# Scan stage of a two-block model: two jobs of ScalarE's strand are given to VectorE

## The reference

```python
def _ssd_chunked(x, dt, log_a, bm, cm):        # chunks of 128 tokens, 8 heads of 64, 2 groups, state 128
    xdt = (x * dt[..., None]).reshape(n, nc, q, h, p)
    acs = jnp.cumsum(log_a.reshape(n, nc, q, h), axis=2)
    seg = acs_h[..., :, None] - acs_h[..., None, :]
    lmat = jnp.exp(jnp.where(tril, seg, -jnp.inf))
    scores = jnp.einsum('nclhd,ncshd->nhcls', c_h, b_h) * lmat
    y_diag = jnp.einsum('nhcls,ncshp->nclhp', scores, xdt)
    ...
    return (y_diag + y_off).reshape(n, t, h, p)

y = unboth(_ssd_chunked(both(xs, xs), ...))    # forward and reversed
y = y + ssd_d.astype(f32)[:, None] * xs        # the D product, per head
```

## Time and profile before

| what | value |
|---|---|
| three runs | 2898.67, 2905.77, 2908.02 us |
| median | 2905.77 us |
| the profiled execution | 2908.02 us, its span 2906.2 us |
| TensorE, VectorE, ScalarE, GpSimd busy | 95%, 59%, 40%, 7% of the span |
| mean granted TensorE clock | 0.974 of full |

### The profile page before, as it was taken

How to read it: one execution, slowest core, us unless ns; L and a number is a source line. 1 busy time by engine, 2 the same in 40 slices (tenths; PEclk the granted TensorE clock), 3 DMA queues, 4 the chain that set the end, 5 groups by cost and what they waited for, 6 DMA issues and landing times.

```text
span 2906.2 us, 41919 instructions
## 1 busy us (share of the span) xinstructions
PE 2748.0 (95%) x16930; PEld 2095.4 (72%) x16930; DVE 1717.6 (59%) x3101; ACT 1163.1 (40%) x2102; POOL 211.3 (7%) x212
## 2 busy tenths in 40 slices
PE   7999997889999999999988999999999998999998
PEld 4888766775766666666645776888888775788887
DVE  4256876665677777767647787533333688433333
ACT  3332654222255565555522328422223327432222
POOL 0000000000011222221200020000000030000000
PEclk9999897999999999999999999999999999999999
DMA  6210001434368899999976340313323250222311
GB/s 234 87 58 23 1 1 47 122 91 157 145 262 341 345 347 354 347 352 342 360 283 233 98 113 1 123 59 128 97 69 121 86 130 15 88 87 86 124 63 69
DMA packets 186543, 442.39 MB, mean 152 GB/s; under 512 B 21284, under 2 KB 110695, under 8 KB 167015
## 3 DMA queue, kind: packets, MB, share of 16 engines
q1 hardware_dynamic: 161862, 396.59, 37.9%
q0 software_dynamic: 24480, 43.04, 5.0%
HBM read 426.43 MB, written 38.29 MB: 160 GB/s over the span
## 4 chain that ended last, share of the span: by engine, by line
PE 78%; DVE 8%; DMA 7%; ACT 4%; issue 2%; POOL 0%; SPq 0%; POOLq 0%; ACTq 0%; DVEq 0%
PE ps L296 18%; PE ps L298 18%; PE ps L297 18%; PE ps L2514 6%; DMA ring<-in_ew 3%; DMA hg<-h_rows,idx 2%; PE ps L2030 2%; PE ps L1514 2%; PE ps L2540 1%; PE ps L2753 1%; PE ps L2234 1%; DVE Pb L3500 1%; PE ps L586 1%; DMA yr<-y_rows 1%; PE ps L3386 1%
## 5 line engine op out<-in xcount | busy, mean ns | idle before, releaser
L2965 DVE TENSOR_TENSOR wf<-ring,wf 128x1024 fp32r<-128x1024 f32 (+1 forms) x152 | 181.6, 1196 | 310.8 <-ACT wf L2961 310.5
L2961 ACT ACTIVATE wf<-ring 128x1024 fp32r<-128x1024 f32 (+1 forms) x152 | 156.8, 1033 | 346.3 <-PE ps L298 346.3
L296 PE MATMUL ps<-hxh,wf 128*128 128x512 f32 (+1 forms) x736 | 279.9, 380 | 2.3 <-DVE hxl L3128 2.3
L297 PE MATMUL ps<-hxl,wf 128*128 128x512 f32 (+1 forms) x736 | 279.5, 380 | 0.0
L298 PE MATMUL ps<-hxh,wf 128*128 128x512 f32 (+1 forms) x736 | 279.5, 380 | 0.0
L2452 DVE TENSOR_TENSOR spA<-ring,spA 128x1024 fp32r<-128x1024 f32 x156 | 184.3, 1220 | 104.9 <-ACT spA L2447 104.8
L2514 PE MATMUL ps<-ring,hdT 128*128 128x512 f32 x520 | 234.8, 594 | 0.8 <-issue 0.8
L2447 ACT ACTIVATE spA<-ring 128x1024 fp32r<-128x1024 f32 x156 | 157.7, 1053 | 57.3 <-DMA ring<-in_ew 50.1
L2452 DVE TENSOR_TENSOR spB<-ring,spB 128x1024 fp32r<-128x1024 f32 x104 | 123.8, 1220 | 70.1 <-ACT spB L2447 70.1
L2514 PEld LDWEIGHTS ps<-ring,hdT 128*128 128x128 f32 x520 | 93.8, 190 | 94.3 <-issue 91.2
L296 PEld LDWEIGHTS ps<-hxh,wf 128*128 128x128 f32 x736 | 138.4, 188 | 29.0 <-DVE hxl L3128 2.8
(11 more groups left out here) (622 smaller groups left out, 6148.8 us busy)
## 6 DMA issues: line engine op xcount, KB each, us to landing
ring<-in_ew SPq DMA_DIRECT2D x65, 2048.0 KB, 12.2
ring<-in_ew SPq DMA_DIRECT2D x65, 1024.0 KB
ring<-in_w_in SPq DMA_DIRECT2D x17, 2048.0 KB, 7.9
ring<-in_w_gate SPq DMA_DIRECT2D x20, 1024.0 KB, 5.5
ring<-in_w_up SPq DMA_DIRECT2D x20, 1024.0 KB, 8.1
ring<-in_w_down SPq DMA_DIRECT2D x16, 1024.0 KB, 5.0
adaw<-in_ada_w SPq DMA_DIRECT2D x24, 512.0 KB, 6.6
ring<-in_w_out SPq DMA_DIRECT2D x6, 2048.0 KB, 8.0
```

The lines of the kernel that those rows point to most:

```text
L296: pe.matmul(o, lhs[0], rhs[0], start=start, stop=False)
L297: pe.matmul(o, lhs[0], rhs[1], start=False, stop=False)
L2961: act.activation(item_part(n)[0], item_raw(n), ACT.Copy).then_inc(*w_hi.inc(n))
L2965: v.tensor_tensor(item_part(n)[1], item_raw(n), f(item_part(n)[0]), ALU.subtract).then_inc(*w_lo.inc(n))
```

## The change

Both jobs leave ScalarE's strand. VectorE makes `lax` with one multiply of 128x1024 (`g128` repeated for 8 heads, times the head's log decay repeated along 128 columns), and the D product with one multiply of 128x512 into the buffer `yo`, which is free once L1037 has read it; x is no longer overwritten. The signals follow: TensorE waits for `lx` from VectorE, and VectorE no longer waits for ScalarE's D product.

```diff
@@ ssd_pe
-                pe.wait_ge(*PA.val(((i - 1, d), "lx")))
+                pe.wait_ge(*PV.val(((i - 1, d), "lx")))
@@ ssd_act
-                if i < 4:
-                    act.wait_ge(*PV.val((u, "xdt")))
-                    for h in range(8):
-                        o = B["xst"][:, 64 * h:64 * h + 64]
-                        m = act.activation(o, o, ACT.Copy, scale=sdd[:, h:h + 1])
-                    m.then_inc(*PA.inc((u, "xd")))
                 yield
                 yield
-            if 1 <= i < 5:
-                at = 16 * ORD[d][i + 1] + 8 * d
-                for h in range(8):
-                    m = act.activation(B["lax"][:, 128 * h:128 * h + 128], C(f"g128_{d}"), ACT.Copy, scale=las[:, at + h:at + h + 1])
-                m.then_inc(*PA.inc((u, "lx")))
@@ ssd_dve
                 if i < 4:
                     v.tensor_tensor(ydst, bA[:, :], yo_, ALU.add).then_inc(*PV.inc((u, "ys")))
                     v.wait_ge(*PV.val((u, "ys")))
-                    v.wait_ge(*PA.val((u, "xd")))
+                    v.tensor_tensor(h8(yo_), h8(xst), bc(sdd[:, :], 64), ALU.mult).then_inc(*V.inc())
+                    v.wait_ge(*V.val())
...
-                v.tensor_tensor(ydst, ydst, xst if i < 4 else yo_, ALU.add).then_inc(*PV.inc((u, "yd")))
+                v.tensor_tensor(ydst, ydst, yo_, ALU.add).then_inc(*PV.inc((u, "yd")))
...
+            if 1 <= i < 5:
+                la = las[:, 16 * ORD[d][i + 1] + 8 * d:16 * ORD[d][i + 1] + 8 * d + 8]
+                v.tensor_tensor(lax.rearrange("p (h s) -> p h s", h=8), bcm(C(f"g128_{d}"), 8), bc(la, 128),
+                                ALU.mult).then_inc(*PV.inc((u, "lx")))
             if x:
                 yield
```

More of the change, by code:

```diff
@@ L902, in _program @@
     s_pe = [Signal(sem(f"ssd_mm{d}"), ssd_keys(d, "xT ex bT ~seg0 ~seg1 ~y ~o st", "bT st")) for d in range(2)]
-    s_act = [Signal(sem(f"ssd_scalar{d}"), [k for k in ssd_keys(d, "xst ex btk ~e0 ~e1 ~xd lx", "btk lx") if k != ((0, d), "lx") and (k[1] != "xd" or k[0][0] < 4)]) for d in range(2)]
-    s_dve = [Signal(sem(f"ssd_vector{d}"), ssd_keys(d, "~gt xdt xde ~sc0 ~sc1 ~yo ~ys ~yd H", "xde H")) for d in range(2)]
+    s_act = [Signal(sem(f"ssd_scalar{d}"), ssd_keys(d, "xst ex btk ~e0 ~e1", "btk")) for d in range(2)]
+    s_dve = [Signal(sem(f"ssd_vector{d}"), [k for k in ssd_keys(d, "~gt xdt xde ~sc0 ~sc1 ~yo ~ys ~yd lx H", "xde lx H")
+                                            if k != ((0, d), "lx")]) for d in range(2)]
     def ssd_pe(pe, d):
@@ L974, in ssd_act @@
         for i in range(6):
-            u, pu, x = (i, d), (i - 1, d), i >= 2
+            u, pu = (i, d), (i - 1, d)
             act.wait_ge(*P.val((u, "xT")))
```

## The result

The changed kernel took 2916.55 us (median of 5, 2914.11 to 2920.84) beside 2902.02 us (5 runs, 2896.44 to 2908.02) for the kernel before. The ratio of their fast runs is 1.0052, 95% interval 1.0040 to 1.0064, so 11.6 to 18.6 us slower. The profiled execution took 2919.35 us (span 2917.6), 11.3 us more than the one of before. The forecast of 2916.0 holds in sign and time. The difference was forecast at 10.2 us; it is 14.5 by the two medians, and most of what follows is about the part that was missing. That the time itself came within 0.6 us is luck in part: it was counted from 2905.77 us, the median of three runs of before, and that of five is 3.75 us lower, about as much as the difference came out too small.

What follows compares the result with a forecast made beforehand. VectorE was taken to set the scan stage's time until TensorE takes over near 369 us. Terms 0.8 + 3.1 + 3.1 + 2.3 = 9.3 us, plus 0.9 for TensorE's clock, gave 10.2 us: 2916.0 us, range 2907 to 2924.

Steps and rivals of the forecast that it cites:

- What bounds the stage: Scan stage: VectorE sets the time from 355.14 until TensorE takes over near 369 us; ScalarE's removed bursts are worth zero.
- The products: On VectorE: 1.13 us for each of eight `lax` multiplies, 0.72 us for each of four D multiplies.
- the dear end of 2.34 us: Upper bound for one `lax` product on VectorE, if two broadcasts should cost; 8.5 us more in the sum.
- Rounds 2 and 3: Units i = 2 and 3, both products in each direction on VectorE: 3.11 us longer each.
- Round 4: Unit i = 4, `lax` products only, no wait in direction 1: 2 x 1.13 = 2.26 us longer.
- Unit 1: Two `lax` products on VectorE, the first starting in its 0.83 us wait before L1052: 0.8 us longer.
- TensorE's clock: New TensorE lulls before L927 and L1101 may drop its clock: 0.3 us for each of three rounds, 0.9 in all.
- The bounds of 0 and 6: Range of the clock term: 0, or 2 us a round, 6 in all, if the clock stays low at L1101, L935 and L1104.
- The heavy price: By the skill's rule on recurring gaps, each of three rounds pays for a fallen clock: the 6 us bound, 2921.1 us.
- The sum: Whole stage: 0.8 + 3.1 + 3.1 + 2.3 = 9.3 us without the clock, 10.2 us with its 0.9.
- Rival 3: TensorE's clock falls in every round and costs in full: 9.3 + 6 = 15.3 us, 2921.1 us; chance 15%.
- Rival 2: The 1.64 us wait at a round's end takes back part of the additions: 3.6 us, 2909.4 us; chance 16%.

Runs made afterwards that it cites:

- `lax` alone: Kernel before with only the `lax` product moved to VectorE, the D product left on ScalarE: 2916.98 us, ratio 1.0046 to before.
- `lax` ahead of the wait: Changed kernel with the `lax` product issued ahead of VectorE's wait for the output matmuls in units 2 to 4: 2912.66 us, ratio 1.0027 to before.
- D alone: Kernel before with only the D product moved to VectorE, `lax` left on ScalarE: 2908.24 us, ratio 1.0018 to before.

## Why the forecast was right, and where it was not

*What bounds the stage:* right. Steps added between VectorE's waits count in full (D: +1.70 us for 1.7 expected), a step removed comes back in full (-4.35), and ScalarE's L1002 bursts are worth 0.0 us in the periods.

*The products:* right. 1.13 for `lax`, 0.73 for D; the dear end of 2.34 us for two broadcast inputs is out. The Trainium skill ("VectorE: DVE Perf Modes", The DRAIN you can't avoid) would have the neighbour wait until the pipe is empty, and adds that an instruction which nothing holds may start earlier; the traces show the second: 1.13 or 1.14 us after the start of an instruction of 1.22, behind every one of these products.

*Rounds 2 and 3:* 3.1 us each, measured 3.11 and 3.12 with the clock held. *Round 4:* 2.3, measured 2.6 to the first multiply, with the new wait of 0.28 us, and 0.1 more to the second: mis-sized by 0.5 in all.

*Unit 1:* 0.8 forecast, 1.45 measured (entry 24.34 against 22.89). The step that failed is "the first product starts in the 0.83 us in which VectorE waited before L1052". That wait stands in one of the five profiles that leave unit 1 as it was, the one in which TensorE had run at half clock longest ahead of it; in the others it is absent and covers nothing. With the low clock there, `lax` alone did pay what was forecast, 0.89 us. I read the clock beside the rows and did not ask whether the wait would be there without it.

*TensorE's clock:* 0.3 us a round, 0.9 in all; the term that was most mis-sized. The first lull came as forecast (1.53 us for 1.6), the second was shorter (0.65 to 0.92 for 1.3), and the clock fell in each of the three rounds. In the rounds it cost 2.2 us in one profile (118.86 against 116.64) and 2.6 in the other, and 3.4 more in the other's entry, where I had looked for nothing: after unit 1 TensorE waits 1.54 us at L928, too. The bounds of 0 and 6 held for the sum, 2.2 and 6.0, but by luck: the upper one was three rounds of 2 us, while one round of each profile paid 2.2 or 2.5, its other two almost nothing, and the entry of the second made up the rest. The Trainium skill ("TensorE: Matmul & The Clock Gate", HAM oscillation) warned of a fall every time round, and these profiles bear it out as to the falls, though its own case has a longer wait in each turn than any lull here. The heavy price that the prediction drew from it did not come every time: it was 0 to 2.5 us a round, since TensorE's own waits for VectorE that come after the fall, 0.92 and 0.40 us, take up the short ones.

*The sum:* clock-free 1.45 + 8.97 = 10.4 us (9.3 forecast), with the clock 12.6 and 16.4 in two profiles. The measured 11.6 to 18.6 holds both. (Against the first profile of before, whose entry was itself 1.3 us longer, the changed kernel's first profile is 11.3 us over in the stage. The two executions also differ by 11.3, but only because 1.2 us gained ahead of the stage are lost behind it.) Rival 3 was right on the falls and wrong on "in full": neither profile of the changed kernel paid in more than one of the three rounds to speak of. The second still reached its 15.3 us, by way of the entry. Rival 2 falls: the wait at a round's end stayed 1.64 us wherever the clock was full or its fall short, since TensorE's queue moved along with VectorE.

*What stays open:* outside the stage the executions drift against each other. `lax` ahead of the wait is 8.1 us behind before at L1473 and ends 0.2 us ahead of it; before itself gains 3.2 us there from one profile to the next. No kernel's own share in that is shown. Nor is it shown what decides whether a lull brings the clock down: the idle matmuls filled both lulls at once, and equal lulls did and did not (see the last section).

## What to carry to other kernels

A chain of waits names the last to arrive, not the one that matters: compare the lag behind the releaser with and without the queue in front, and the cover shows itself. Work moved off an idle engine onto the one that paced these rounds cost its whole start-to-start time, unless it was put into a wait, where the same instruction was free. And price the lulls that a delay opens on TensorE: read from the trace whether the clock falls at such a lull and what waits TensorE still has after it, which take a short fall up, and if a slack is to cover a term, check that it was not itself made by a low clock.

## What the runs showed of the hardware

- A 128x1024 f32 multiply with both inputs broadcast takes 1.22 us on VectorE, as one with no such inputs.
- In every round of both profiles of the changed kernel TensorE's clock fell to half. Its lulls there were 1.52 or 1.53 us in front of L928 and 0.65 to 0.92 us in front of L1096 of direction 0; in one round the fall came before the second of them. Twenty idle matmuls a round, which fill both, kept it at full.
- The length of the lulls alone doesn't tell whether it falls. With `lax` ahead of the wait, 0.39 and 0.92 us in the same two places came with a fall in two rounds, 0.46 and 0.92 with none in the other. With `lax` alone it fell in one round behind a single lull of 0.92 us (by 336.5 us), in the next only behind 0.92, 0.92 and 0.40. D alone (0.43 or 0.44 and 0.92 us, 3.5 us apart, twice with 0.40 behind them) and before (0.70 and 0.40, in its last round 0.44 and 0.92) had none in any round.
- After a fall in unit 1 or later the clock came back within some 3 to 10 us, at another distance in each execution, so that the same kernel's round takes 30.73 or 33.21 us.
